# Output projection of the prompt rows in three rounded products, and the expert weights placed around its operands

## What is computed

```python
merged = sigmoid(gate_a) * (o_attn @ w_pa) + sigmoid(gate_b) * (o_conv @ w_pb)
x = x + gate1 * (merged @ w_o)                       # w_o: 1024 x 1024
h = rmsnorm(x, g_ffn) * (1 + scale2) + shift2
lg = h @ w_rg + b_rg                                 # top-1 of 4 groups
le = h @ w_re + b_re                                 # top-2 of 8 experts in the group
y = einsum('btef,efd->btd', silu(a) * b * combine[..., None], w_down_e)
return rmsnorm(x + gate2 * y, g_final)
```

## Time and profile before

| | |
|---|---|
| median of 3 runs | 782.72 us (782.16 to 785.43) |
| span of the profiled execution (no other time of it is given) | 780.6 us |
| TensorE busy | 694.1 us, 89% of the span |
| VectorE busy | 319.5 us, 41% |
| ScalarE busy | 165.6 us, 21% |
| GpSimd busy | 124.9 us, 16% |
| moved by DMA | 198.48 MB, mean 254 GB/s |
| chain of waits, share of TensorE | 82% |
| last input product, output projection, first expert start | 414, 423, 513 us |

### The profile page before, as it was taken

One profiled execution on the slowest core, in us unless ns is written; L12 is line 12 of the kernel. 1 busy time (PEld: TensorE's weight loads), 2 busy tenths in 40 slices (PEclk: granted clock), 3 DMA queues, 4 the chain that ended last, 5 costly groups with the idle time before them and its releaser, 6 DMA issues.

```text
span 780.6 us, 12215 instructions
## 1 busy us (share of the span) xinstructions
PE 694.1 (89%) x5015; PEld 531.6 (68%) x5015; DVE 319.5 (41%) x707; ACT 165.6 (21%) x323; POOL 124.9 (16%) x189
## 2 busy tenths in 40 slices
PE   3889999999999999999999999779999987788810
PEld 1588898889898989999996555555555554555500
DVE  3442223136878754222334755425333222112235
ACT  4342123111264332211110211111111111001001
POOL 3300003010023001000000100123333322322112
PEclk9999999999999999999999999679999999889975
DMA  9934565864145256511107954779999999999873
GB/s 336 347 142 163 218 266 221 314 238 145 57 161 166 78 196 217 198 55 55 55 31 266 418 207 153 251 294 400 417 412 413 411 412 418 417 415 416 349 299 145
DMA packets 40435, 198.48 MB, mean 254 GB/s; under 512 B 8210, under 2 KB 8394, under 8 KB 24756
## 3 DMA queue, kind: packets, MB, share of 16 engines
q1 hardware_dynamic: 31088, 175.42, 57.8%
q0 software_dynamic: 8352, 21.81, 8.0%
q10 hardware_dynamic: 940, 0.47, 0.2%
HBM read 188.54 MB, written 17.40 MB: 264 GB/s over the span
## 4 chain that ended last, share of the span: by engine, by line
PE 82%; DMA 6%; DVE 4%; issue 4%; ACT 2%; POOL 1%; SPq 1%; POOLq 0%; DVEq 0%; ACTq 0%
PE bank L1699 30%; PE bank L1944 16%; PE bank L1899 7%; PE bank L1966 7%; PE bank L1842 4%; DMA arena<-in_w_ada 3%; PE bank L1937 2%; PE bank L1839 2%; PE bank L1596 2%; PE bank L1735 2%; PE bank L1798 2%; DMA arena<-in_w_in 1%; PE bank L1860 1%; PE bank L1639 1%; PE bank L1961 1%
## 5 line engine op out<-in xcount | busy, mean ns | idle before, releaser
L1699 PE MATMUL bank<-h_parts,w_parts 128*128 128x260 f32 x2112 | 267.5, 286 | 2.1 <-issue 1.5
L1699 PEld LDWEIGHTS bank<-h_parts,w_parts 128*128 128x128 f32 x2112 | 257.9, 189 | 11.2 <-issue 9.6
L1944 PE MATMUL bank<-arena,arena_b 128*64 128x256 f32 x704 | 89.9, 412 | 13.6 <-issue 9.2
L1944 PEld LDWEIGHTS bank<-arena,arena_b 128*64 128x64 f32 x704 | 57.6, 148 | 39.6 <-issue 12.5
L1088 DVE TENSOR_TENSOR w_parts<-arena,w_parts 128x1024 fp32r<-128x1024 f32 x46 | 56.2, 1221 | 60.5 <-ACT w_parts L905 60.3
L1449 DVE TENSOR_TENSOR arena_b<-bank,arena_b 128x128 f32<-128x128 f32 x32 | 9.3, 292 | 129.8 <-ACT arena_b L1017 127.1
L836 POOL DMA_INDIRECT y_scratch<-arena_b x32 | 33.2, 1037 | 162.3 <-DVE arena_b L1474 154.8
L905 ACT ACTIVATE w_parts<-arena 128x1024 fp32r<-128x1024 f32 x46 | 48.4, 1053 | 49.1 <-DMA arena<-in_w_in 34.7
L1899 PE MATMUL bank<-arena,arena_b 128*128 128x512 f32 x128 | 56.7, 597 | 0.0
L1944 PE MATMUL bank<-arena_b 128*64 128x256 f32 x320 | 40.1, 407 | 6.4 <-issue 5.2
L1966 PE MATMUL bank<-arena,arena_b 128*64 128x512 f32 x176 | 42.3, 593 | 0.8 <-DVE arena_b L1455 0.8
(11 more groups left out here) (306 smaller groups left out, 785.5 us busy)
## 6 DMA issues: line engine op xcount, KB each, us to landing
arena<-in_w_gate_up SPq DMA_DIRECT2D x44, 1024.0 KB, 28.3
arena<-in_w_in SPq DMA_DIRECT2D x46, 512.0 KB, 5.8
arena<-in_w_ada SPq DMA_DIRECT2D x22, 1024.0 KB, 7.4
arena<-in_w_down SPq DMA_DIRECT2D x20, 1024.0 KB
arena_b<-in_w_gate_up SPq DMA_DIRECT2D x20, 1024.0 KB
arena_b<-in_w_down SPq DMA_DIRECT2D x20, 512.0 KB
arena_b<-in_x_prompt SPq DMA_DIRECT2D x8, 512.0 KB, 5.9
arena_b<-q_scratch POOLq DMA_DIRECT2D x3, 1024.0 KB, 5.7
```

The costliest lines, as they stand in the source:

```text
L1699: ins = pe.matmul(ps[s][:, 0:HALF], w_parts[:, n % 2, wp, k], h_parts[:, hp, k, s * HALF:(s + 1) * HALF], start=(k == 0 and hp == 1), stop ...
L1944: ins = pe.matmul(ps[2 + b][R * hh:R * hh + R, 0:2 * P], hTe[:, b, c * P + jj * R:c * P + jj * R + R], w_gu[slot][jj][:, c, :, hh * P:(hh ...
```

## The change

The prompt rows' output projection is no longer made of float32 products. As in the input projection, both operands are split into a rounded part and a rest (float32r), and three products are added in one bank: rest of merged by rounded w_o, rounded by rounded, rounded merged by rest of w_o. The product of the rests is left out. The samples' 8 rows keep float32 products with the unsplit `w_o`; their merged features go to a small tensor `m_s`.

ScalarE makes the rounded parts (`merged_rounded`, `wo_rounded`), VectorE the rests (`merged_rest`, `wo_rest`). A merged feature's sum is written over one of its sigmoid inputs, so ScalarE's sigmoids now wait for `s_mlo` and not `s_mrg`. `wo_lo[c]` overwrites `wo[c]` in place, after the samples' product. For the new tensors the reloaded x moves from X to the end of SPLIT, and the 6 gate/up and 7 down places are laid out anew; all down weights now come as two loads of 512 KiB (before, four of the seven places took one of 1 MiB). SyncE's order and waits change with them. Semaphores of early stages are merged into one (`s_cond`), which changes no wait.

```diff
+        wo_hi = [rounded("wo_hi0", layout["SPLIT"] + 8 * D, [KD, 512]), rounded("wo_hi1", layout["SPLIT"] + 4 * D, [KD, 512])]
+        wo_lo = [rounded("wo_lo0", wo0_at, [KD, 512]), wo_lo1]
+        m_hi = rounded("m_hi", layout["QK"], [KD, TP])
+        m_lo = rounded("m_lo", layout["X"] + 2 * T, [KD, TP])
...
-        x = cube(region("X", 0, 5 * D), 5)
+        x = cube(region("SPLIT", 17 * D, 5 * D), 5)
+        xh = cube(region("X", 0, 5 * D), 5)
...
+        gu_at = [[split_at(12, 2), spare(4 * D, 2 * D)], [split_at(17, 2), split_at(8, 2)], [split_at(10, 2), wo0_half(0)],
+                 [wo0_half(1), split_at(4, 2)], [split_at(6, 2), region("X", 0, 2 * D)],
+                 [region("X", 2 * D, 2 * D), split_at(19, 2)]]
+        dn_at = [[split_at(14, 1), split_at(15, 1)], [split_at(16, 1), split_at(21, 1)],
+                 [spare(6 * D, D), spare(7 * D, D)], [split_at(0, 1), split_at(1, 1)],
+                 [region("X", 4 * D, D), region("QK", D, D)], [spare(0, D), spare(D, D)], [spare(2 * D, D), split_at(22, 1)]]
...
@@ SyncE, after the reload of x
-            for e in range(3):
-                for half in range(2):
-                    load_gate_up(e, e, half)
-                load_down(e, e, 0)
-            sp.wait_ge(s_h2, 2)
-            load_gate_up(4, 4, 1)
-            load_down(4, 4, 1)
+            sp.wait_ge(s_gfu, 1)
+            load_gate_up(0, 0, 0)
+            load_down(0, 0, 0)
+            load_down(1, 1, 0)
+            sp.wait_ge(s_wom[1], 1)
+            load_down(0, 0, 1)
+            keep_x(0)
+            sp.wait_ge(s_h2, 2)
+            load_gate_up(0, 0, 1)
+            for part in range(2):
+                load_down(2, 2, part)
+            sp.wait_ge(s_xw[0], 16)
+            load_down(1, 1, 1)
+            keep_x(1)
+            keep_x(2)
+            sp.wait_ge(s_h2, 6)
+            sp.wait_ge(s_xw[1], 32)
+            load_gate_up(1, 1, 0)
+            keep_x(3)
             sp.wait_ge(s_wom[0], 5)
+            load_gate_up(1, 1, 1)
             for half in range(2):
-                load_gate_up(3, 3, half)
+                load_gate_up(2, 2, half)
+            load_gate_up(3, 3, 0)
             sp.wait_ge(s_wom[1], 5)
-            load_down(3, 3, 0)
+            load_gate_up(3, 3, 1)
+            for part in range(2):
+                load_down(3, 3, part)
             keep_x(4)
...
-            sp.wait_ge(s_hg[0], 16)
...
@@ ScalarE, behind the sigmoids
+            def merged_rounded(f):
+                act.wait_ge(s_mrg, f + 1)
+                act.activation(m_hi[:, f], sig[:, f % 2, 0:TP], ACT.Copy).then_inc(s_mhi, 1)
+            def wo_rounded(c):
+                for k in range(0, KD, 2):
...
+                    act.activation(wo_hi[c][:, k:k + 2], wo[c][:, k:k + 2], ACT.Copy).then_inc(s_wohi, 1)
...
+            wo_rounded(0)
+            merged_rounded(KD - 1)
+            wo_rounded(1)
@@ VectorE
+            def wo_rest(c):
+                dve.wait_ge(s_wom[c], 1)
+                for k in range(0, KD, 2):
+                    dve.wait_ge(s_wohi, 4 * c + k // 2 + 1)
+                    dve.tensor_tensor(wo_lo[c][:, k:k + 2], wo[c][:, k:k + 2], wo_hi[c][:, k:k + 2], ALU.subtract
+                                      ).then_inc(s_wolo, 1)
...
+            merged_rest(KD - 1)
+            wo_rest(0)
+            wo_rest(1)
@@ TensorE
+            def with_rounded(n, c):
+                bank = ps[2 + 2 * (n % 2) + c]
+                at_least(pe, s_x2, 2 * (n - 2) + c + 1 if n >= 2 else 0)
+                for k in range(KD):
...
+                    for part in (m_lo, m_hi):
+                        pe.matmul(bank[:], part[:, k, RB[n] * P:(RB[n] + 1) * P], wo_hi[c][:, k],
+                                  start=(k == 0 and part is m_lo), stop=False, skip_group_check=True)
+            def with_rest(n, c):
+                bank = ps[2 + 2 * (n % 2) + c]
+                for k in range(KD):
...
+                    ins = pe.matmul(bank[:], m_hi[:, k, RB[n] * P:(RB[n] + 1) * P], wo_lo[c][:, k], start=False,
+                                    stop=(k == KD - 1), skip_group_check=True)
...
             project_samples()
-            project(1, 0)
-            project(1, 1)
+            for c in range(2):
+                with_rounded(1, c)
+            for c in range(2):
+                with_rest(1, c)
+            project(2, 0)
             router(0)
-            for n in range(2, 5):
+            project(2, 1)
+            router(1)
+            ranks(0)
+            ranks(1)
+            for n in range(3, 5):
                 project(n, 0)
                 router(n - 1)
                 project(n, 1)
-                if n == 2:
-                    ranks(0)
                 ranks(n - 1)
```

More of the change, by code:

```diff
@@ L445, in hybrid_step @@
         s_yfirst = sem("s_yfirst")
-        s_xw = sem("s_xw")
+        s_xw = [sem(f"s_xw{i}") for i in range(3)]
+        s_mhi = sem("s_mhi")
+        s_mlo = sem("s_mlo")
+        s_wohi = sem("s_wohi")
+        s_wolo = sem("s_wolo")
         s_xl = sem("s_xl")
@@ L643, in _ @@
                     load_down(e, 0, 0)
+                    load_down(e, 0, 1)
                 sp.wait_ge(s_moe, 1)
```

154 lines of the change are left out of this document (86 added, 68 removed).

## The result

The changed kernel takes **787.78 us** (median of 4 runs, 784.72 to 789.13) against 782.75 for the kernel before (4 runs, 782.16 to 785.43): a ratio of 1.0063, 95% interval 1.0038 to 1.0087. The same kernel again, with other runs of the kernel before (782.27), gave 786.92 and 1.0064 (1.0042 to 1.0086). It is slower by 0.6%; 781.5, with a range to 787.5, was forecast.

A forecast was written before the change was run, and what follows sets the result against it. The stream of expert-weight loads was taken as the bound: +11.4 us of moved loads, -12.8 of filled idle time, +0.2 for the later release make -1.2, so span 779.4 and time 781.5; range 775.5 to 787.5.

The forecast's parts named there:

- The products: Output projection: rounded products at 217 ns each, 5.2 us a block; eight blocks give TensorE back 14 us.
- VectorE's rests and the samples' rows: VectorE makes w_o's rests from about 423.6 to 433.5; the samples' rows, begun at 423.4 before, start only then.
- TensorE's three waits: TensorE waits before row block 2 (3 us), block 1's router and the ranks (4.4 us); row block 3 starts at 460.4.
- The release: The last row block's first half ends at 481.0 (before 480.76) and releases most places of expert weights.
- 4.7 MB moved behind it: Early loads ahead of 481 fall from 11.0 to 6.3 MB; the 4.7 MB moved cost 11.4 us of stream.
- The idle time that they fill: Idle DMA time from 481 to 540, 13.3 us less 0.5 that stays idle, is filled by the new queue.
- Rival (d): Experts' start: the first gather takes 9.6 us behind a full queue, 4.3 us stay idle: 785.8 or 787.5; chance 0.17.
- (a): Row block 3: the clock stays full, release at 479.2, idle time counts by bytes (15.0 us): 778.0; chance 0.18.
- (b): Output products overlap down to their weight loads, 122 ns each; the release is 6 us earlier: 775.5; chance 0.05.
- (c): TensorE's saving comes through whole; experts and stream start 8 x 1.75 us earlier: 769; chance 0.05.
- (e): Down weights: each of the 20 more loads costs the stream 0.33 us, 6.6 us in all: 788; chance 0.05.
- The signs: Wrong if row block 3 starts before 457, DMA share stays below 0.95 (482 to 520), or expert gaps vanish before 700.

The follow-up runs named there:

- hold8: The changed kernel, with the load queue waiting for the first gather before its last eight early loads: 788.1 us, +5.8 against the kernel before.
- before_no_hold: The kernel before, without the load queue's wait for the first gather ahead of its last four early loads: 784.5 us, ratio 1.0037.
- layout_only: The changed kernel's places, loads and order, but float32 output products from unsplit operands, without parts or rests: 791.3 us, ratio 1.0107.
- reorder: The changed kernel, with ranks behind row block 3's first half and each router behind the half block not needing it: 788.1 us, +5.9.

## Why the prediction was wrong

- **The products: slightly off.** 232 ns apart at full clock (the 29 steps from 423.91 to 430.66 take 6.75 us), near the upper end of 235 and not the 217 taken. A half block costs 5.6 us, not 5.2; eight win 11 us.
- **VectorE's rests and the samples' rows: right.** Rests at 1.15 us intervals (1.22 taken) from 423.5 to 432.6, the samples' first copy at 432.60 (433.5).
- **TensorE's three waits: right in place.** Row block 2 at 436.17 (436.9), the membership at 458.21 + 0.19 (459.5), row block 3 at 459.44 (460.4), at half clock first: 0.43 us between products. The gaps were 1.4 and 2.7 us, not 3 and 4.4.
- **The release: right, in part by luck.** 481.59, forecast 481.0. VectorE's chain ended 1.1 us early (458.40 for 459.5), and from the start of row block 3 TensorE took 22.0 us instead of 20.6 with the dearer products (459.44 to 481.40); the two errors nearly cancelled.
- **4.7 MB moved behind it: right**, by the windows.
- **The idle time that they fill: this is the step that failed.** The text said that "after 481 the new queue has no wait that outlasts its backlog", and took 12.8 us of idle time as filled. 3.3 MB, 8.0 us, were. The backlog did run out, at about 521.7, because the first expert and so the first reload (522.80) were late. And that came from a price left at the old one: the gather at 3.0 us, as with DMA nearly free, though the same paragraph filled the queue in front of it. Measured 6.65.
- **Rival (d) was the case**, with 0.17. Its mechanism was shown by the runs: hold8 empties the queue and the gather takes 3.04; before_no_hold fills it in the kernel before and it takes 6.30, for 2.2 us; and in thirteen of the fourteen profiles the first to last gate/up takes 224.4 to 226.4 us (230.2 in hold8). Its size was another matter. It gave 785.8 to 787.5 with 6.6 us of delay; 3.6 were measured, and by (d)'s own sum only 1.3 of these stay idle: 782.8, or 784.5 by share. That is near the profiled 784.7 and 3.3 us or more below the median of 787.8. What that sum left out is the second dip, from 528 to 532 (233 GB/s): it ends the idle time at the first reload. So that (d)'s figure lies next to the median is in part luck.
- **(a) and (b)** fell with the half clock behind the gap and the 232 ns. **(c)**: TensorE's saving came through for 3.9 us at the release (layout_only), and the new order had cost 4.5 there. **(e)**: about 1 us for the 14 loads tested.
- **The signs.** None of the three signs of being wrong came: row block 3 at 459.44, a DMA share of 0.99 from 482 to 520, gaps between experts after 700. What failed is an item of the other list, "DMA full from 482 to the last load": the dips from 520 to 532 lie just behind the stretch that the sign watched.
- **The frame** was too narrow. I held the release of the places against idle DMA time. What the runs follow is the first expert's start: from the first reload on both kernels load the same 80.7 MB of weights (52 gate/up halves, 25 downs). reorder moved the release by 6.4 us and the time by nothing.

What stays open is the 2 us or so by which the medians differ more than the profiles, so about half of the slowdown, and why the profiles reach S up to 4 us apart. S is 419.5 on average in the three profiles of the kernel before and its variants and 420.4 in the eleven others, so 1 us may lie ahead of S; so few profiles with such a spread don't show it.

## What to carry to other kernels

When a change fills idle DMA time, ask what short transfer on the critical path will now queue behind it, and price that transfer from a row with a full queue; here 3.6 us were lost on a gather of rows that came while bulk weights were streaming. Holding bulk loads back isn't free either: held ones return as a longer stream. And follow a gain to the event that the later work is chained to (here the first reload), not to the first event that moves.

## What the hardware showed that I had not expected

- A gather of 0.26 MB took 2.98 to 3.04 us from issue to the first transpose with the DMA engines idle or nearly so (three profiles) and 6.3 to 7.8 with bulk loads in flight (eleven profiles).
- VectorE's subtraction of 128x1024 with a rounded result took 1.22 us alone and about 3.4 beside GpSimd's own of the same kind, which took 3.29: eight pieces on one engine took 9.17 us, five and three on two took 12.35.
- Rounded products of 512 columns with a new weight load each are issued 0.232 us apart at full clock and 0.43 at half.
